# Seven block products instead of eight for the gate and up projections of 12 of 16 experts

## The reference

```python
def expert_choice_moe(x, w_router, w_gate_up, w_down):
    cap = CAPACITY_FACTOR * S // N_EXPERTS                    # 2 * 1024 // 16 = 128 tokens
    aff = jax.nn.softmax((x @ w_router).astype(jnp.float32), axis=-1)
    gates, idx = lax.top_k(jnp.swapaxes(aff, 1, 2), cap)
    xs = x[bi, idx]
    g, u = jnp.split(jnp.einsum('becd,edf->becf', xs, w_gate_up), 2, axis=-1)
    out = jnp.einsum('becf,efd->becd', jax.nn.silu(g) * u, w_down) * gates[..., None]
    return jnp.zeros_like(x).at[bi, idx].add(out)
```

## Time and profile before

| | |
|---|---|
| median of 3 runs | 4085.08 us (4083.64 to 4085.57) |
| profiled execution, span | 4083.8 us |
| PE busy | 3849.1 us (94%) |
| DVE busy | 1537.7 us (38%) |
| ACT busy | 1076.9 us (26%) |
| POOL busy | 376.3 us (9%) |
| mean granted PE clock | 0.977 |
| expert stages | some 2090 to 2840 us and 3320 to 4060 us of the span |

### The profile page before, as it was taken

The page is one execution under the profiler, slowest core; times in us unless marked ns, Lnnn a source line. Parts: engine busy times, 40 slices in busy tenths (PEclk is TensorE's granted clock), DMA queues, the critical chain, the costliest instruction groups (busy, mean ns, idle before and its releaser), DMA issues. The chain is left out here.

```text
span 4083.8 us, 64554 instructions
## 1 busy us (share of the span) xinstructions
PE 3849.1 (94%) x27772; PEld 2109.9 (52%) x27772; DVE 1537.7 (38%) x3250; ACT 1076.9 (26%) x2335; POOL 376.3 (9%) x533
## 2 busy tenths in 40 slices
PE   8998999898989799999979999998999989999998
PEld 4555755757575644545544444443444444444443
DVE  2233335565656511135657111113356547111113
ACT  2334223434343311025631000003343421000003
POOL 3340002111111000000100000000000000000000
PEclk9999999999999999999989999999999989999999
DMA  4101101000000042020049999997211148999997
GB/s 107 32 22 39 33 27 47 9 22 9 27 4 22 4 143 78 11 62 1 1 173 320 313 321 306 329 316 256 84 36 31 52 170 315 313 322 308 328 317 247
DMA packets 320588, 567.29 MB, mean 139 GB/s; under 512 B 53504, under 2 KB 127392, under 8 KB 320304
## 3 DMA queue, kind: packets, MB, share of 16 engines
q1 hardware_dynamic: 304832, 506.01, 36.8%
q0 software_dynamic: 9504, 34.61, 3.5%
q10 hardware_dynamic: 5968, 22.55, 1.4%
HBM read 514.85 MB, written 48.23 MB: 138 GB/s over the span
## 5 line engine op out<-in xcount | busy, mean ns | idle before, releaser
L3541 PE MATMUL bank<-ring,m_picked_T 128*128 128x512 f32 x2048 | 899.5, 597 | 4.1 <-ACT m_picked_T L3624 4.1
L3541 PEld LDWEIGHTS bank<-ring,m_picked_T 128*128 128x128 f32 x2048 | 389.7, 192 | 482.7 <-issue 477.3
L3541 PE MATMUL bank<-ring,m_hidden_T 128*128 128x512 f32 x1024 | 455.3, 593 | 0.0
L3541 PEld LDWEIGHTS bank<-ring,m_hidden_T 128*128 128x128 f32 x1024 | 189.6, 190 | 215.5 <-issue 215.5
L3790 DVE TENSOR_TENSOR m_hidden<-m_hidden,bank 128x512 f32<-128x512 f32 x64 | 44.0, 687 | 508.6 <-ACT m_hidden L3630 508.6
L1562 PE MATMUL bank<-hnT,first_block 128*128 128x336 f32 (+3 forms) x544 | 183.2, 489 | 8.0 <-PEq L101 7.3
L3630 ACT ACTIVATE m_hidden<-bank 128x512 f32<-128x512 f32 x64 | 38.2, 597 | 540.2 <-PE bank L3541 540.1
L241 PE MATMUL bank<-xT,first_block 128*128 128x512 f32 x352 | 152.4, 593 | 2.8 <-ACT l_i L3269 1.7
L3920 POOL DMA_INDIRECT y_rows<-m_ys,m_tokens x30 | 47.7, 1588 | 1112.3 <-DVE m_ys L3805 1047.7
L2825 PE MATMUL bank<-xT,a_weights 128*128 128x512 f32 x320 | 142.3, 595 | 0.8 <-ACT xT L2681 0.8
L1562 PEld LDWEIGHTS bank<-hnT,first_block 128*128 128x128 f32 x544 | 102.7, 194 | 66.6 <-issue 19.4
...
## 6 DMA issues: line engine op xcount, KB each, us to landing
ring<-in_moe_w_gate_up SPq DMA_DIRECT2D x512, 512.0 KB, 7.5
ring<-in_moe_w_down SPq DMA_DIRECT2D x256, 512.0 KB, 4.6
...
```

Of the source, the lines that this page charges most:

```text
L3541: m = pe.matmul(banks[j][:, :], lhsT[:, (i % 8) * P:(i % 8 + 1) * P], ring[:, i, j, :], start=i % 8 == 0, stop=i % 8 == KD - 1)
```

## The change

For experts 3 to 14 of each layer (`SEVEN`) the tokens are cut into two halves of 64 and the gate-and-up matrix into four quarters of 512 x 1024 (rows by columns), and the product of the two 2 x 2 block matrices is made from seven block products in place of eight. `product` makes one: four contraction blocks, and for each two matmuls of 64 stationary columns and 512 moving ones, whose outputs go to partitions 0 to 63 and 64 to 127 of one bank. The token sums are made by GpSimd (`sum_tokens`, four operations of 128x256). Of the four weight sums, each four operations of 128x1024, the first (quarter 1 minus quarter 0, in place) is made by GpSimd (`differ`), the other three (`sum_second`, `sum_third`, `sum_fourth`) by DVE, into the space of `X`. `join` on DVE combines the products with 128x512 operations and applies the gate. The first product of expert e + 1 is made ahead, in two parts within expert e. ACT does both token copies, both hidden copies and both output scalings. `sync` loads whole rows of 4 KB for these experts, in groups of four slabs, each group behind the product that frees it. Experts 0 to 2 and 15 keep the old form.

```diff
...
+        SEVEN = range(3, NE - 1)
+        PRODUCTS = ("11", "s2t2", "s3t3", "s1t1", "22t4", "12b21", "s4b22")
...
+        EARLY = 4
...
         def slab(e, i):
 
+            if e in SEVEN and i < 16:
+                down, right = ((0, 0), (0, 1), (1, 1), (1, 0))[i // 4]
+                at = (half_rows * down + i % 4) * P
+                w = io["moe_w_gate_up_2"][layer][e][at:at + P, FF * right:FF * right + FF]
+                return w.rearrange("p (x c) -> p x c", x=2)
...
+            for e in SEVEN:
+                sp.wait_ge(w_summed.sem, w_summed_at(e, "t3_3"))
+                sp.wait_ge(made.sem, made_at(e, "11"))
+                for i in range(4):
+                    load(e + 1, i)
+                for i in range(20, SLABS):
+                    sp.wait_ge(used.sem, used_at(e - 1, i + 1))
+                    load(e, i)
+                sp.wait_ge(made.sem, made_at(e, "s1t1"))
+                for i in range(4, 8):
+                    load(e + 1, i)
+                sp.wait_ge(made.sem, made_at(e, "12b21"))
+                for i in range(12, 16):
+                    load(e + 1, i)
+                sp.wait_ge(made.sem, made_at(e, "s4b22"))
+                for i in range(8, 12):
+                    load(e + 1, i)
+                for i in range(16, 20):
+                    sp.wait_ge(used.sem, used_at(e, i + 1))
+                    load(e + 1, i)
+            for i in range(20, SLABS):
+                sp.wait_ge(used.sem, used_at(NE - 2, i + 1))
+                load(NE - 1, i)
...
+            def product(bank, tokens_, weights, parts=(0, 4)):
+
+                for j in range(*parts):
+                    for half in range(2):
+                        m = pe.matmul(bank[tok[half], :], tokens_(j), weights(j)[:, 512 * half:512 * half + 512],
+                                      start=j == 0, stop=j == 3)
+                return m
...
+            def first_product(e, lo, hi):
+
+                if lo == 0:
+                    pe.wait_ge(x_even.sem, e + 1)
+                    pe.wait_ge(x_odd.sem, e + 1)
+                    landed_all(e, 0)
+                    if e > SEVEN[0]:
+                        pe.wait_ge(joined.sem, joined_at(e - 1, "u3"))
+                m = product(first_bank(e), x_quarter(e, 0, 0), weight(0), (lo, hi))
+                if hi == 4:
+                    m.then_inc(*made.up())
+
+            def four_products(e):
+                if e > SEVEN[0]:
+                    pe.wait_ge(joined.sem, joined_at(e - 1, "21"))
+                pe.wait_ge(w_summed.sem, w_summed_at(e, "t2_3"))
+                pe.wait_ge(x_summed.sem, x_summed_at(e, "s2"))
+                product(ps[1], summed(2), t2).then_inc(*made.up())
+                pe.wait_ge(w_summed.sem, w_summed_at(e, "t3_3"))
+                product(third_bank(e), summed(1), t3).then_inc(*made.up())
+                product(ps[3], summed(0), weight(1)).then_inc(*made.up())
+                pe.wait_ge(joined.sem, joined_at(e, "u2"))
+                pe.wait_ge(w_summed.sem, w_summed_at(e, "t4_3"))
+                product(ps[1], x_quarter(e, 1, 1), t2).then_inc(*made.up())
+
+            def fifth_product(e):
+
+                pe.wait_ge(kept.sem, e - SEVEN[0] + 1)
+                landed_all(e, 3)
+                product(first_bank(e), x_quarter(e, 0, 1), weight(3)).then_inc(*made.up())
+
+            def last_product(e):
+
+                pe.wait_ge(joined.sem, joined_at(e, "u4"))
+                pe.wait_ge(x_summed.sem, x_summed_at(e, "s4"))
+                landed_all(e, 2)
+                product(ps[3], summed(3), weight(2)).then_inc(*made.up())
...
+            def turn_half(e, i):
+
+                pe.wait_ge((x_even, x_odd)[i].sem, e + 2)
+                pe.wait_ge(acted.sem, 4 * e + 2 * i + 2)
+                for b in range(4):
...
+                if e in SEVEN:
+                    first_product(e, 2 * i, 2 * i + 2)
+                    return
...
+            turn_tokens(0)
+            for e in range(NE):
+                if e in SEVEN:
+                    if e == SEVEN[0]:
+                        first_product(e, 0, 4)
+                    four_products(e)
+                    turn_tokens(e + 1)
+                    fifth_product(e)
+                    turn_half(e, 0)
+                    last_product(e)
+                    ahead(e + 1, 0)
+                    turn_half(e, 1)
+                    ahead(e + 1, 1)
+                    pe.wait_ge(h_even.sem, 2 * e + 2)
+                else:
...
+            def keep_first(e):
+
+                if e > SEVEN[0]:
+                    ac.wait_ge(acted.sem, 4 * e - 1)
+                ac.wait_ge(made.sem, made_at(e, "11"))
+                ac.activation(first_kept[:, :], first_bank(e)[:, :], ACT.Copy).then_inc(*kept.up())
+
+            def sigmoid_half(e, i):
+                if i == 0:
+                    ac.wait_ge(joined.sem, joined_at(e, "21"))
+                    ac.activation(hid[:, 512:1024], c21, ACT.Sigmoid).then_inc(*sig.up())
+                else:
+                    ac.wait_ge(joined.sem, joined_at(e, "11"))
+                    ac.activation(hid[:, 0:512], first_kept[:, :], ACT.Sigmoid).then_inc(*sig.up())
...
+                if e in SEVEN:
+                    copy_tokens(e + 1)
+                    for i in range(2):
+                        sigmoid_half(e, i)
+                        copy_half(e, i)
+                    if e + 1 in SEVEN:
+                        keep_first(e + 1)
...
                 ac.activation(ys[:, 0:512], ps[6][:, :], ACT.Copy, scale=gates[:, e:e + 1]).then_inc(*y_even.up())
+                if e in SEVEN:
+                    ac.activation(ys[:, 512:], ps[7][:, :], ACT.Copy, scale=gates[:, e:e + 1]).then_inc(*y_odd.up())
+                if e + 1 == SEVEN[0]:
+                    keep_first(e + 1)
...
+            def sum_second(e, j):
+
+                if e == SEVEN[0] and j == 0:
+                    ve.wait_ge(grown.sem, NT)
+                    ve.wait_ge(rows_out.sem, 16)
+                ve.wait_ge(landed[8 + j].sem, 16 * (e + 1))
+                ve.wait_ge(differed.sem, 4 * (e - SEVEN[0]) + j + 1)
+                if e > SEVEN[0]:
+                    ve.wait_ge(made.sem, made_at(e - 1, "22t4"))
+                ve.tensor_tensor(t2(j), quarter(2, j), quarter(1, j), ALU.subtract).then_inc(*w_summed.up())
+
+            def sum_third(e, j):
+                ve.wait_ge(w_summed.sem, w_summed_at(e, f"t2_{j}"))
+                ve.tensor_tensor(t3(j), t2(j), quarter(0, j), ALU.subtract).then_inc(*w_summed.up())
+
+            def sum_fourth(e, j):
+
+                ve.wait_ge(made.sem, made_at(e, "s2t2"))
+                ve.wait_ge(landed[12 + j].sem, 16 * (e + 1))
+                ve.tensor_tensor(t2(j), t2(j), quarter(3, j), ALU.subtract).then_inc(*w_summed.up())
+
+            def sum_pairs(e):
+                for j in (0, 2):
+                    sum_second(e, j)
+                    sum_second(e, j + 1)
+                    sum_third(e, j)
+                    sum_third(e, j + 1)
+
+            def join(e):
+
+                ve.wait_ge(made.sem, made_at(e, "s2t2"))
+                ve.wait_ge(kept.sem, e - SEVEN[0] + 1)
+                ve.tensor_tensor(u2[:, :], ps[1][:, :], first_kept[:, :], ALU.add).then_inc(*joined.up())
+                sum_fourth(e, 0)
+                sum_fourth(e, 1)
+                ve.wait_ge(made.sem, made_at(e, "s3t3"))
+                ve.wait_ge(joined.sem, joined_at(e, "u2"))
+                ve.tensor_tensor(u3[:, :], third_bank(e)[:, :], u2[:, :], ALU.add).then_inc(*joined.up())
+                sum_fourth(e, 2)
+                sum_fourth(e, 3)
+                ve.wait_ge(made.sem, made_at(e, "s1t1"))
+                ve.wait_ge(joined.sem, joined_at(e, "u3"))
+                ve.tensor_tensor(c22[:, :], ps[3][:, :], u3[:, :], ALU.add).then_inc(*joined.up())
+                ve.wait_ge(made.sem, made_at(e, "s1t1"))
+                ve.tensor_tensor(u2[:, :], ps[3][:, :], u2[:, :], ALU.add).then_inc(*joined.up())
+                ve.wait_ge(made.sem, made_at(e, "22t4"))
+                ve.tensor_tensor(c21, u3[:, :], ps[1][:, :], ALU.subtract).then_inc(*joined.up())
+                ve.wait_ge(joined.sem, joined_at(e, "21"))
+                ve.tensor_tensor(c22[:, :], c22[:, :], c21, ALU.mult).then_inc(*acted.up())
+                ve.wait_ge(sig.sem, 2 * e + 1)
+                ve.wait_ge(*acted.now())
+                ve.tensor_tensor(hid[:, 512:1024], hid[:, 512:1024], c22[:, :], ALU.mult).then_inc(*acted.up())
+                ve.wait_ge(made.sem, made_at(e, "12b21"))
+                ve.tensor_tensor(first_kept[:, :], first_bank(e)[:, :], first_kept[:, :],
+                                 ALU.add).then_inc(*joined.up())
+                ve.wait_ge(sig.sem, 2 * e + 2)
+                ve.tensor_tensor(hid[:, 0:512], hid[:, 0:512], first_kept[:, :], ALU.mult).then_inc(*acted.up())
+                ve.wait_ge(made.sem, made_at(e, "s4b22"))
```

(31 more changed lines are left out.)

125 lines of the change are left out of this document (96 added, 29 removed).

## The result

Five runs of the changed kernel have a median of 4100.53 us (4098.91 to 4110.40), five of the kernel before 4085.08 us. The ratio is 1.0044, 95% interval 1.0033 to 1.0055. The forecast was 4056 us with a range of 4037 to 4092: the time lies outside, on the slow side.

What follows compares the result with a forecast made beforehand. PE alone was taken to bound the stage; 22 experts gaining 1.15 us and two gaining 2.0 take 29 us off the profiled 4083.8 us span, 1.3 us under the median: forecast 4056 us, range 4037 to 4092.

Steps and rivals of the forecast that it cites:

- PE's work: Tensor engine, changed experts: seven block products of 3.43 us where eight were, 3.43 us less for an expert.
- change of form: PE switching between full-width and paired 64-column records: 0.15 to 0.19 us lost each, 1.3 us an expert.
- the prediction's floor: PE time of one changed expert without waits: 42.96 - 3.43 + 1.3 = 40.8 us.
- The order at the port: SBUF port, DVE's line 4045 against GpSimd's first difference: either may go first; middle gain taken, 1.15 us an expert.
- vector first: At the SBUF port line 4045 precedes GpSimd's first difference; cost 0.1 to 0.9 us, an expert gains 1.3 to 2.0.
- rival 1: SBUF port: DVE goes ahead of GpSimd in every changed expert; 4037 to 4052 us, middle 4042; chance 0.22.
- the term for line 4058: M4, DVE's last gate operation before PE's transposes: done by 26.0 when PE wants it at 26.3, nothing lost.
- GpSimd first: At the SBUF port the first difference precedes line 4045; PE loses 1.75 us, an expert gains 0.3; throughout, chance 0.20.
- Rival 3: SBUF port: GpSimd goes ahead and a late difference also delays line 4058; slower, middle 4103 us; chance 0.16.
- The start of the differences: GpSimd, after quarter 1's load priced as a lone slab (3.8 to 3.9 us): port asked for at 14.4 or later.
- The gather: Token gather for the next products: lands at 13.8, PE wants it at 14.0; wait of 0 to 0.3 us.
- Rival 4: PE: halves don't run side by side, a product costs 6.9 us; kernel some 4610 us; chance 0.02.

Runs made afterwards that it cites:

- ungrouped run: Changed kernel with joins in PSUM and the early gather together, token transposes not yet regrouped; no PE waits left within a changed expert: 4040.3 us, ratio 0.9890 to before.

## Why the prediction was wrong

**PE's work: right.** A product takes 3.43 us (2423.17 - 2419.74 in the timeline of the ungrouped run), a change of form 0.15, and an expert without waits 40.77 us against the 40.8 of the sum. From the first down product of expert 2 to that of expert 15, in the profiled executions, the run with joins in PSUM and early gather is 26 us a layer under before, 52 in all, where the prediction's floor gave 24 x 2.15 = 52.

**The order at the port.** I took it to fall out both ways and the middle of the two prices. Line 4045 was first in all 24 experts, with 0.69 us: that is "vector first" throughout, the condition of rival 1, for which I had 4037 to 4052 us. So the middle of the two orders was the wrong term, but it is not what made the kernel slower. A `differ` takes 2.35 us or 2.8, less than the 0.7 more that I named. Line 4048 I had done in time in this order, at no cost. In twelve of the 22 experts with differences it took 1.81 to 2.87 us, and PE waited 0.45 us an expert for it.

**The step that failed** is the term for line 4058. The prediction says of "vector first": "Later ones meet in slack. Cost with product 5's wait: 0.1 us", and of "GpSimd first" that M4 is done in time. I walked the four differences to their end in one ordering only. In "GpSimd first" PE is 1.75 us late, so line 4058 is asked for at some 25.2, just behind the last difference. In "vector first" PE is on time and asks from 23.4 on, and the same differences end at 25.0 to 25.8 by the prediction's own numbers: the whole of the slack of 0.3 us is gone, and more. PE waits 1.56 us an expert for it on the mean. The run with quarter 1 first has nearly the forecast's start and shows this chain: in most of its experts the differences end at 25.5 or 25.6, and line 4058, asked for at 23.5, is done at 26.1, in the two experts 14 at 24.2. Rival 3 named this place and a lateness of 0.8 to 1.9 us, but only for "GpSimd first", and I gave it 0.16. That its 4103 us is close to the 4100.5 measured is luck: it holds the 1.75 us of "GpSimd first", which did not occur, and lacks the gather's wait and the slow clock. The run with one operand in PSUM gives the price of this meeting alone.

**The start of the differences: wrong, without effect.** I priced the load of quarter 1 as a lone one, 3.85 us. Eight slabs are queued ahead of it and the scatter and the gather move at the same time. Its slabs land 8.35 us behind their issue in the median, 6.7 in the run that puts them ahead of four of these. The landings of all slabs in the changed kernel are

```profile
DMA to landing us min/median/max: 3.2/7.7/16.3
```

and the differences begin at 17.5 us in the median, not at 14.4. I had the row that speaks against the lone load and used it only for rival 1. So the 0.3 us between the two orders, on which the whole forecast rested, did not exist.

**The gather: mis-sized.** I took 0 to 0.3 us, it was 0.83. Its issue was not the reason: it comes 4.0 us behind the down product, where I had 3.6 + 0.7. It lands later than in the earlier trace rows:

```profile
DMA to landing us min/median/max: 8.6/10.7/12.6
```

9.5 us became 10.7, beside slabs that now come eight at a time. In the run with quarter 1 first the four down slabs are issued behind it and no longer ahead, it lands in 8.1 us in the first layer (5.8 to 8.5), and its wait is gone.

**Not in the sum at all:** the slow clock behind PE's waits (0.58 us an expert), and 2.3 us a layer in the last expert, whose gate is wanted 7 us earlier by PE and stands behind row statistics on ScalarE. (The first changed expert of a layer, 1.5 to 1.7 us later than with the joins in PSUM, is the same wait behind line 4058.) Rival 4's sum takes 22 experts where 24 have the new products; it would be some 4660 us. It did not occur.

Together: -51.9 us for PE's work, +71.0 for the waits and the clock from expert 2 to 15, which is the difference between this profile and that of the run without waits, and +4.6 for the wait in the last experts. The sum is +23.7, and that is what the two stages grew by from expert 2 on; the span grew by 24.9.
